# Down-projection weight sums formed by accumulating DRAM transfers instead of GpSimd, token sums on VectorE, and squares added one tile later

## What is computed

```python
def squared_relu_mlp(h, w_up, w_down):
    a = jax.nn.relu(h @ w_up)          # 1024 -> 4096
    return (a * a) @ w_down            # 4096 -> 1024
...
h = h + squared_relu_mlp(rms_norm(h, mlp_norm[i]), mlp_w_up[i], mlp_w_down[i])
```

## Time and profile before

| | |
|---|---|
| median of 3 runs | 2099.44 us (2092.85, 2099.44, 2100.04) |
| profiled execution | 2094.79 us, span 2093.0 us |
| TensorE / VectorE / ScalarE / GpSimd busy | 95% / 71% / 43% / 22% |
| up pairs | 388 to 656.4 us of the span |
| down steps | 656.4 to 914.4 us |
| last down tiles | 914.4 to about 1014 us |

### The profile page before, as it was taken

How to read it: one execution, slowest core, us unless ns; L and a number is a source line. 1 busy time by engine, 2 the same in 40 slices (tenths; PEclk the granted TensorE clock), 3 DMA queues, 4 the chain that set the end, 5 groups by cost and what they waited for, 6 DMA issues and landing times. The chain is left out here.

```text
span 2093.0 us, 26629 instructions
## 1 busy us (share of the span) xinstructions
PE 1985.8 (95%) x9870; PEld 1627.9 (78%) x9870; DVE 1496.2 (71%) x2475; ACT 904.3 (43%) x1725; POOL 450.2 (22%) x358
## 2 busy tenths in 40 slices
PE   6999999999998899998899999989989999999997
PEld 4877787888886778786788888778877777888775
DVE  7278877688887889888689895774363456777644
ACT  4266544655555344432531232741242235555422
POOL 2023223233225455333400010000020012222200
PEclk9999999999999999999999999999999999999998
DMA  3202001555655223433231165233022211111312
GB/s 133 67 21 102 22 31 31 192 187 189 211 187 190 94 91 117 146 127 111 61 121 41 41 161 143 73 105 153 33 103 71 73 54 39 35 30 41 116 41 91
DMA packets 62576, 202.55 MB, mean 97 GB/s; under 512 B 7280, under 2 KB 12016, under 8 KB 61168
## 3 DMA queue, kind: packets, MB, share of 16 engines
q1 hardware_dynamic: 58416, 184.77, 26.2%
q0 software_dynamic: 1584, 7.29, 1.8%
q10 hardware_dynamic: 2448, 8.79, 1.1%
HBM read 156.84 MB, written 36.70 MB: 92 GB/s over the span
## 5 line engine op out<-in xcount | busy, mean ns | idle before, releaser
L177 PE MATMUL banks<-u2H,wH 128*128 128x512 f32 (+1 forms) x704 | 260.8, 370 | 3.9 <-POOL u2L L439 2.1
L178 PE MATMUL banks<-u2L,wH 128*128 128x512 f32 (+1 forms) x704 | 257.4, 366 | 0.0
L179 PE MATMUL banks<-u2H,wL 128*128 128x512 f32 (+1 forms) x704 | 257.1, 365 | 0.0
L1117 POOL TENSOR_SCALAR logits<-logits,stat 128x256 f32<-128x256 f32 (+3 forms) x96 | 121.4, 1278 | 341.3 <-DVE stat L992 341.3
L172 DVE TENSOR_TENSOR wL<-raw,wH 128x1024 fp32r<-128x1024 f32 x101 | 125.6, 1244 | 74.7 <-ACT wH L167 74.4
L2395 DVE SCALAR_TENSOR_TENSOR conv_out<-conv_in,par,conv_out 128x1295 f32<-128x1295 f32 x108 | 162.7, 1565 | 0.6
L177 PEld LDWEIGHTS banks<-u2H,wH 128*128 128x128 f32 x704 | 133.9, 190 | 27.0 <-issue 3.7
L177 PE MATMUL banks<-kpH,formH 128*128 128x512 f32 x336 | 134.2, 399 | 20.4 <-DVE hm L2061 14.4
L179 PEld LDWEIGHTS banks<-u2H,wL 128*128 128x128 f32 x704 | 133.8, 190 | 21.5
L178 PEld LDWEIGHTS banks<-u2L,wH 128*128 128x128 f32 x704 | 133.8, 190 | 20.1 <-issue 0.2
L167 ACT CAST wH<-raw 128x1024 fp32r<-128x1024 f32 x101 | 105.7, 1047 | 88.6 <-DMA raw<-in_wstream 86.6
(11 more groups left out here) (406 smaller groups left out, 5350.1 us busy)
## 6 DMA issues: line engine op xcount, KB each, us to landing
raw<-in_wstream SPq DMA_DIRECT2D x101, 512.0 KB, 3.6
sraw<-in_sstream SPq DMA_DIRECT2D x58, 512.0 KB, 4.5
mod_w<-in_mod_w SPq DMA_DIRECT2D x48, 512.0 KB, 3.8
hidden_scratch<-hid SPq DMA_DIRECT2D x64, 256.0 KB, 2.3
kpR<-hidden_scratch SPq DMA_DIRECT2D x24, 512.0 KB, 4.6
side_sum<-side_tap POOLq DMA_DIRECT2D x11, 647.5 KB, 5.7
gt<-gates_scratch SPq DMA_DIRECT2D x8, 640.0 KB, 3.9
h<-in_x SPq DMA_DIRECT2D x4, 1024.0 KB, 10.4
```

What stands on the lines that cost most here:

```text
L177: first = pe.matmul(out, aH, bH, start=start, stop=False, skip_group_check=more)
L178: pe.matmul(out, aH, bL, start=False, stop=False, skip_group_check=more)
L179: return first, pe.matmul(out, aL, bH, start=False, stop=stop, skip_group_check=more)
L1117: m = pool.tensor_scalar(src, src, stat[:, SUM, k % 3, hs:hs + 1], None, ALU.mult)
```

## The change

1. **Weight sums.** The host lays the down weights out as four block arrays (`sblocks`: W11, W12, W21, W22; 15 steps x 128 x 512 floats, 3.75 MiB each). During up pairs 1 to 12 GpSimd issues transfers from DRAM to DRAM that make the four sums of all steps in `sums_scratch`: four steps at a time, in six parts, one part per pair, two groups side by side. Of the eight transfers of a group four are copies and four accumulate onto the copy. Before part p a GpSimd wait asks that part p-1 of that group has landed. GpSimd no longer works in the down steps.
2. **Form loads.** The SyncE queue loads each form of a down step by itself (`form_load`, 128 rows of 1 to 2 KB), nine products ahead, into a ring of ten places; the four new places are those of `sraw`. The SyncE loop now runs over slots instead of steps, so its other transfers are interleaved with these.
3. **Token sums.** X1, X2, X3 of each kp go from GpSimd to VectorE (`kp_sum_of`), and the tables are rewritten (`prepare`).
4. **Squares.** In the last down tiles VectorE adds the square of tile j-1 after the residual of tile j, and the second kind of square too for tiles 0 to 11 (`G_DVE = 12`), which GpSimd did.

```diff
+        def presum_step(pool, group, part):
+            lo, hi = PRESUM_GROUP * group, min(PRESUM_GROUP * group + PRESUM_GROUP, DOWN_STEPS)
...
+            if part or group >= 2:
+                pool.wait_ge(turn, count + (PRESUM_DONE[part - 1] if part else 0))
+            if part == 0:
+                pool.dma_start(R1, A21).then_inc(turn, 16)
+                pool.dma_start(R3, A11).then_inc(turn, 16)
+            if part == 1:
+                pool.dma_start(R1, A22, accum_op=ALU.add, max_dma_last_dim=8192).then_inc(turn, 16)
+                pool.dma_start(R3, A21, accum_op=ALU.add, max_dma_last_dim=8192).then_inc(turn, 16)
+            if part == 2:
+                pool.dma_start(R2, R1).then_inc(turn, 16)
+            if part == 3:
+                pool.dma_start(R2, A11, accum_op=ALU.add, max_dma_last_dim=8192).then_inc(turn, 16)
+            if part == 4:
+                pool.dma_start(R4, R2).then_inc(turn, 16)
+            if part == 5:
+                pool.dma_start(R4, A12, accum_op=ALU.add, max_dma_last_dim=8192).then_inc(turn, 16)
...
+        def form_load(sp, f):
...
+            if f >= EXTRA0:
+                sp.wait_ge(prod_done, step_done(LAST_USE[9]))
+            elif g >= RING:
+                sp.wait_ge(forms_begun, f - RING + 2)
+            elif g in (2, 3, 6, 7, 8, 9):
+                sp.wait_ge(forms_begun, UP_PRODUCTS - {2: 4, 3: 3, 6: 2, 7: 1, 8: 0, 9: -1}[g])
+            else:
+                sp.wait_ge(form_ready, UP_PRODUCTS - (FORMS if g < 2 else 0))
...
+        prepare(0, -1, 1, {0: (X11, X1), 1: (X2, X22), 2: (X3, X21), 3: (X4,)},
+                {0: (SUM1, SUM2, SUM3, SUM4), 1: (X11, X1), 2: (X2, X22, X3), 3: (X21, X4)})
...
+            for s in range(PRODUCTS):
+                n, i = divmod(s, FORMS)
...
+                if s == UP_PRODUCTS - 9:
+                    form_load(sp, UP_PRODUCTS)
+                if UP_PRODUCTS - 9 < s + 1 and s + 9 < PRODUCTS and s + 9 > UP_PRODUCTS:
+                    form_load(sp, s + 9)
...
+                for kp in SP_KP.get((n, i), ()):
                     kp_load(sp, kp)
...
-            for n in range(STEPS):
-                for kp in POOL_KP.get(n - 1, ()):
-                    kp_sums(pool, kp)
...
+            for n in range(PAIRS):
+                form_sums(pool, n)
+                for group, part in PRESUMS[n - 1] if 0 < n <= len(PRESUMS) else ():
+                    presum_step(pool, group, part)
...
-            for j in range(15):
+            for j in range(G_DVE, 15):
                 add(j)
...
             for j in range(14):
                 residual(j)
-                add(j)
+                if j:
+                    add(j - 1)
+                    if j - 1 < G_DVE:
+                        add_scaled(j - 1)
```

More of the change, by code:

```diff
@@ L1458, in form_free, with weight @@
                 eng.wait_ge(units_begun, base + 3 + f // 2)
[L1460 to L1462 removed]
+        def weight(n, kind):
+            return sraw[:, 2 * (n % 2) + kind // 2, TN * (kind % 2):TN * (kind % 2) + TN]
         def weight_loaded(eng, n, row):
             eng.wait_ge(sraw_loaded[2 * (n % 2) + row], 16 * (n // 2 + 1 + SRAW_FREE))
[L1468 to L1473, removed]
[L1474 to L1482 removed]
@@ new lines, in form_sums @@
+        def form_sums(pool, n):
+            f = FORMS * n
+            for row in range(2):
+                weight_loaded(pool, n, row)
+            form_free(pool, f + 1)
+            pool.tensor_tensor(form(formR, f + 1), weight(n, W21), weight(n, W22), ALU.add).then_inc(form_sum, 1)
+            form_free(pool, f + 2)
+            pool.wait_ge(form_sum, 4 * n + 1)
+            pool.tensor_tensor(form(formR, f + 2), form(formR, f + 1), weight(n, W11), ALU.add).then_inc(form_sum, 1)
+            form_free(pool, f + 3)
+            pool.wait_ge(form_sum, 4 * n + 2)
+            pool.tensor_tensor(form(formR, f + 3), form(formR, f + 2), weight(n, W12), ALU.add).then_inc(form_sum, 1)
+            form_free(pool, f + 4)
+            pool.tensor_tensor(form(formR, f + 4), weight(n, W11), weight(n, W21), ALU.add).then_inc(form_sum, 1)
@@ L1484, in form_source @@
         def form_source(f):
             n, i = divmod(f, FORMS)
-            return weight(n, *PLAIN[i]) if i in PLAIN else form(formS, f)
+            return weight(n, PLAIN[i]) if f < UP_PRODUCTS and i in PLAIN else form(formR, f)
         def form_high(act, f):
@@ L1619, in build @@
+        prepare(4, 3, 0, {0: (X11,), 1: (X1,), 2: (X2, X22), 3: (X3, X21), 5: (X4,)},
+                {0: (SUM1,), 1: (SUM2,), 2: (SUM3,), 3: (SUM4, X11), 4: (X1, X2), 5: (X22,), 6: (X3, X21), 7: (X4,)})
         PREP = {4: 5, 5: 6, 6: 7, 7: 8, 8: 9, 9: 10, 10: 11}
         for n, kp in PREP.items():
[L1621 to L1624 removed]
@@ L2111, in mlp_dve @@
                     finish_modulations()
+            add(13)
             split_lo(dve, E0)
@@ L3398, in layout @@
                 block = down[P * (lo + 12 * half):P * (hi + 12 * half), P * m:P * m + P]
-                steps[st, row, :, 512 * half:512 * half + P * (hi - lo)] = pack_units(block)[0]
-    out["sstream"] = np.concatenate([up[4:], steps.reshape(-1, P, D)])
+                steps[2 * row + half, st, :, 0:P * (hi - lo)] = pack_units(block)[0]
+    out["sblocks"] = steps
+    out["sstream"] = up[4:]
     out["x"] = chunked(a["x"][0].T)
```

215 lines of the change are left out of this document (104 added, 111 removed).

## The result

The changed kernel takes 2114.60 us in the median of 4 runs (2110.29 to 2117.33), the kernel before 2096.14 (2092.04 to 2100.04). The ratio is 1.0083, 95% interval 1.0063 to 1.0103: 0.8% slower, where 2074 us were forecast. All of the miss lies in one stretch, and the windows of the changed kernel show it. Columns are as in the earlier trace rows; the five stretches are the first 12 up pairs (but for the last 1.5 us of the twelfth), the last two pairs, all 14 together, the down steps, and the last tiles.

A forecast was written before the change was run, and what follows sets the result against it. TensorE was taken to bound the up pairs, VectorE, partly stretched by GpSimd, the down steps. 2094.8 - 14.7 (down steps with transition) - 8.0 (last tiles) + 2 (up-pair transfers) = 2074 us; range 2060 to 2108.

The forecast's parts named there:

- the part on the up pairs: Up pairs: DRAM transfers mostly hidden, a part may land 17.4 us late before TensorE stands; cost 2 us.
- The budget of engine time: Twelve up pairs: 113 us of loads and spills plus 120 of sums against 228.5 + 17.4, so nothing lost.
- the low end: Up pairs: cheaper transfer estimate, 2.7 us per MiB copied and 5.3 accumulated, 120 us for the sums, nothing lost.
- The slower rival: Up pairs: GpSimd waits for DRAM landings, delaying sums and then TensorE; costs from 133 us of transfers, 2140 at high end; chance 0.23.
- VectorE stays the bound: Down steps: VectorE's instructions not much faster without GpSimd, only the last tiles gain; 2087 us, chance 0.17.
- The transition does not stall: Up pairs to down steps: kp 0 comes earlier or the copy gets through, 6.4 us less; 2067 us, chance 0.08.
- The change misses its mark: Down steps: VectorE is held by its own chain of highs and lows; 2094 to 2100 us, chance 0.04.
- Transition: Pair 13 into step 0: late kp 0 load stalls TensorE 3.6 us before product 3; step 0 6.4 us late.
- Down steps: Down steps: VectorE, freed of stretching by GpSimd, lets 258.0 us become 243.3 including 6.4 for the transition: -14.7.
- Form loads: Down steps: 105 smaller loads replace 30, with 6.8 us at the narrowest against landings of 3.6 to 4.5; hidden.
- Last tiles: Last down tiles: VectorE's 9.7 us per two tiles fits under TensorE's 10.9, the wait for the split goes: -8.0 us.

The follow-up runs named there:

- copies_only: The changed kernel with all accumulating transfers left out, only the copies between DRAM tensors kept: 2078.4 us, up pairs 280.0 us.
- no_transfers: The changed kernel without its DRAM copies and accumulations, the sums' forms loaded from plain weight blocks: 2066.8 us, up pairs 272.3 us.
- early_kp: The changed kernel with the load of kp 0 one slot earlier in SyncE's order, ahead of the third form's load: 2107.6 us.
- gpsimd_busy: The kernel no_transfers with 98 unread GpSimd adds, one per product of the first 14 down steps: 2090.0 us, down steps 254.9 us.
- adds_small: The changed kernel with its accumulating transfers cut to descriptors of 4 KB instead of 8 KB: 2117.6 us.

## Why the prediction was wrong

**The step that failed** is in the part on the up pairs: "What hides a late landing is GpSimd's idle time ... So a part may be 17.4 us late before TensorE stands", with "The other transfers are delayed little". I worked out how late the *sums* may be. They were never what TensorE waited for: GpSimd waited for their landing 6.9 us in two times. What was late were the small transfers that share the 16 engines, and for those the allowance is not 17.4 us but 6.8 - 4 = 2.8 us for one modulation load in three. With the price of a MiB right (5.5 and 3.1 us against 5.3 and 2.7) and the sum of work right (126 us against 120), the term was 2 us and measured 318.0 - 267.8 less the transition's 4.5: some 45.7. The budget of engine time, 113 + 120 against 228.5 + 17.4, asked whether everything gets through in the stretch; it did. It doesn't ask whether each load gets through in the 6.8 us that it has. The budget was also too small by its own rows: with the DMA share of 0.58 in the earlier trace rows the other transfers need 133 us in 228.5, not 113, and the low end would have been 133 + 120 - 246 = 7 us over, where nothing was said to be lost. That is not the miss: it is 7 us of 45.7.

The evidence I used against it was a median over 90 us: a 512-KB load took 4.4 us in a window where the accumulations had 41.1% of the engines. In the up pairs, with 43 to 84% in the windows of accumulation, the median load took 10.5 to 21.7 us. The median of that window was no bound for a load that is issued right behind the transfer.

**The rivals.** The slower rival had the right side and the right source, the transfers, but the wrong chain (GpSimd's wait for the landing) and the wrong threshold: by it nothing is lost under 133 us of engine time, and at 126 us 45.7 were. copies_only loses 8 at 46 us. A piece of it exists in another form, GpSimd held 14.4 us in issuing. *VectorE stays the bound* is refuted by the down steps (236.0 us), *The transition does not stall* by 3.92 us, *The change misses its mark* by 687 ns. The figures that the prediction took from the two pages of the Trainium skill, "DMA: Bandwidth & Descriptors" and "Collectives: The Full Stack" (4.9 and 9.8 us per MiB), are both too high for this case, which measured 3.1 and 5.5. Their verdict "slower" (2159 us) would have been right for the wrong reason.

**Transition.** Forecast 6.4: stall 3.6, measured 3.92; cost 4.5 us in no_transfers, 5.3 in the changed kernel by the length of pair 13, and 7.2 by early_kp. Right in place, chain and nearly in size.

**Down steps.** Without the transition 236.9 forecast, 236.0 measured, in part by luck: the first step took 0.9 us more than forecast and the second 0.9 less. That VectorE's stretching by GpSimd was the cause is shown by gpsimd_busy.

**Form loads.** Hidden as forecast: the loads land in 2.7 us in the median, and TensorE waits for no form.

**Last tiles.** -8.0 forecast; -7.1 in the profile and -7.8 alone.

Without the up pairs' term the sum would have been 2072 us, and no_transfers took 2066.8. Of the 5.3 us between them the transition gives 1.9, the down steps (234.8 us there) 2.1, and an earlier start of the up pairs 1.3.

**What stays open**: how exactly an engine shares its time between the two queues, and so why a load beside an accumulation takes 10 us and more. Beside the two copies of part 4 the queue rows from 499 to 505.5 us tell a good deal:

```profile
q0 software_dynamic: 48, 2.10, 94.5%
q1 hardware_dynamic: 14, 0.02, 0.9%
```

2 MiB went in 32 packets of 64 KB (the other 16 are of a few bytes), each of which held an engine 6.5 x 16 x 0.945 / 32 = 3.07 us. The load issued at 499.77 moved nearly nothing until both copies were through. Beside accumulations, in packets of 8 KB, the two kinds mix. The queue rows from 482 to 487.5 us:

```profile
q0 software_dynamic: 124, 0.88, 77.3%
q1 hardware_dynamic: 125, 0.51, 24.3%
```

These are 108 packets of 8 KB (and 16 small ones), 0.63 us each, against 125 of 4 KB, 0.17 us each. If an engine took one of each in turn, the 8 packets of 4 KB that each engine has for a 512-KB load would need some 8 x 0.80 = 6.4 us, and the other loads in SyncE's queue come on top. This is an estimate; the trace doesn't say which engine a packet was on. "DMA: Bandwidth & Descriptors" ("Queues, rings and completion order") of the Trainium skill says that an engine goes round its queues and changes only when a whole packet of typically 9 to 17 descriptors is through. That would fit long waits too; no run here tells the two apart, since adds_small was held by its issue and no run cut the copies into smaller packets.

## What to carry to other kernels

Before putting bulk transfers beside a tuned stage, list every small transfer of the stage with its allowance (issue to use, less its landing time) and ask what the smallest of them is; a budget of bandwidth over the stage does not answer that. A load whose result nobody needs soon still stops whoever consumes it in order: here modulations that TensorE doesn't need stopped the add that it does. Put bulk transfers where the DMA share is low (0.07 to 0.27 in the attention stage), and check there too which load somebody waits for.

## What the runs showed of the hardware

- Accumulating in DRAM took 5.5 us of all 16 engines per MiB and a plain DRAM copy 3.1; the rows of transfers through SBUF gave 5.3 and 2.7.
- GpSimd can be held in issuing accumulations, and its next sums with it: the fourth 1-MiB one in a row, with rows of 8 KB, waited 14.4 us, with rows of 4 KB the second waited 11.2. That a full queue holds it is not shown.
- A 512-KB load took 10.8 us where it took 4, beside two accumulations (median of the three loads from 476 to 498 us) as well as right behind two copies (499.77 us), though the DMA share over the whole stage was only 0.83.
- The copies' 64-KB packets held an engine 3.07 us each, and a load issued behind them got 0.9% of the engines for 6.5 us.
- 98 GpSimd adds that nobody needed cost the down steps 20 us, through VectorE's instructions with two operands in SBUF: 0.28 us more for a low of a form, none for the add with an operand in PSUM.
